# Where the halves of split weights and of the activations lie, modulo 128 bytes

## The reference

```python
x = first_block(x, c, ...)     # modulation from c, indexed attention, stick-breaking attention,
                               # gated merge, then peer_ffn: keys pick 16 experts per head
x = second_block(x, mem, ...)  # conv + blocked attention + gated linear attention,
                               # cross attention on mem, then a convolved gated FFN of width 2752
```

```python
proj = hn @ w_in[l]                                  # many column blocks: w_qi, w_qb, w_g, ...
qh = (h @ w_q)                                       # w_pq
pre = jnp.einsum('cd,chkd->chk', hc, u[ec])          # computed here for all 16384 experts: u
return jnp.einsum('chk,chkd->cd', coef, v[ec])       # likewise: v, with most coefficients zero
u = causal_dwconv(h @ w_up, ...); ... @ w_down       # w_up, w_dn
```

## Time and profile before

| what | value |
|---|---|
| median of three runs | 1450.76 us (1448.74 to 1456.02) |
| the profiled execution, its own time | 1450.47 us |
| its span, first to last instruction | 1448.7 us |
| granted TensorE clock, mean | 0.988 of full |
| PE busy | 1401.2 us, 97% of the span |
| DVE, ACT, POOL busy | 1097.8, 836.1, 360.9 us |
| share of PE in the chain that ended last | 81% |

### The profile page before, as it was taken

The page is one execution under the profiler, slowest core; times in us unless marked ns, Lnnn a source line. Parts: engine busy times, 40 slices in busy tenths (PEclk is TensorE's granted clock), DMA queues, the critical chain, the costliest instruction groups (busy, mean ns, idle before and its releaser), DMA issues.

```text
span 1448.7 us, 25878 instructions
## 1 busy us (share of the span) xinstructions
PE 1401.2 (97%) x10406; PEld 1301.1 (90%) x10406; DVE 1097.8 (76%) x1903; ACT 836.1 (58%) x1447; POOL 360.9 (25%) x227
## 2 busy tenths in 40 slices
PE   7999999899998999999999999999999999899997
PEld 5998899899998999999988888887889899799997
DVE  7788887567889888999756666677667667797762
ACT  4554774444454677777645445465546666776651
POOL 3216101234445100000032222344322221433200
PEclk9999999899999999999999999999999999999999
DMA  9757775455664544444557666665666536285630
GB/s 386 269 190 268 247 240 176 161 159 179 190 184 146 174 148 147 147 146 146 154 179 221 192 193 196 212 196 181 194 200 245 186 107 199 75 260 176 193 114 30
DMA packets 73721, 268.24 MB, mean 185 GB/s; under 512 B 8401, under 2 KB 9730, under 8 KB 72834
## 3 DMA queue, kind: packets, MB, share of 16 engines
q1 hardware_dynamic: 71280, 256.41, 56.1%
q10 hardware_dynamic: 1426, 7.56, 1.5%
q0 software_dynamic: 896, 2.62, 0.5%
HBM read 262.88 MB, written 3.67 MB: 184 GB/s over the span
## 4 chain that ended last, share of the span: by engine, by line
PE 81%; DVE 12%; ACT 4%; issue 1%; DMA 1%; POOL 1%; DVEq 0%; ACTq 0%; POOLq 0%
PE bank L611 80%; DVE split L1825 3%; DVE ada_acc L1860 2%; ACT split L1295 1%; DVE PR L2275 1%; DMA ringb<-in_w_ada 1%; DVE PR L2272 1%; POOL H L2644 0%; PE bank L784 0%; POOL split L2617 0%; DVE H L2366 0%; DVE PR L2280 0%; DMA vecs<-in_vecs 0%; DVE PA L2076 0%; DVE MH L1927 0%
## 5 line engine op out<-in xcount | busy, mean ns | idle before, releaser
L611 PE MATMUL bank<-H,split 128*128 128x256 f32 x5928 | 732.8, 282 | 15.9 <-DVE split L1825 7.7
L611 PEld LDWEIGHTS bank<-H,split 128*128 128x128 f32 x5928 | 710.2, 189 | 23.5 <-DVE split L1825 9.9
L1295 ACT CAST split<-ringb 128x1024 fp32r<-128x1024 f32 x350 | 365.9, 1047 | 284.5 <-PE bank L611 270.7
L2617 POOL TENSOR_TENSOR split<-ringb,split 128x1024 fp32r<-128x1024 f32 x91 | 229.0, 2517 | 665.7 <-ACT split L1295 665.7
L611 PE MATMUL bank<-split,H 128*128 128x512 f32 (+1 forms) x1728 | 391.1, 388 | 3.3 <-DVE H L2366 1.8
L1825 DVE TENSOR_TENSOR split<-ringb,split 128x1024 fp32r<-128x1024 f32 x259 | 330.9, 1280 | 77.5 <-ACT split L1295 77.4
L611 PEld LDWEIGHTS bank<-split,H 128*128 128x128 f32 x1728 | 321.3, 188 | 71.2 <-POOL split L2617 2.5
L2366 DVE TENSOR_TENSOR H<-PR,H 128x256 fp32r<-128x256 f32 x128 | 137.1, 1074 | 105.5 <-ACT H L1634 105.4
L1825 DVE TENSOR_TENSOR split<-far,split 128x1024 fp32r<-128x1024 f32 x77 | 99.7, 1303 | 33.5 <-ACT split L1295 33.4
L1295 ACT CAST split<-far 128x1024 fp32r<-128x1024 f32 x89 | 92.7, 1047 | 55.1 <-PE bank L611 43.9
L1610 ACT ACTIVATE PR<-bank 128x512 f32<-128x512 f32 (+31 forms) x59 | 28.7, 486 | 76.3 <-PE bank L611 76.3
(11 more groups left out here) (298 smaller groups left out, 1264.0 us busy)
## 6 DMA issues: line engine op xcount, KB each, us to landing
ringb<-in_u SPq DMA_DIRECT2D x128, 512.0 KB, 3.7
ringb<-in_v SPq DMA_DIRECT2D x128, 512.0 KB, 4.4
ringb<-in_w_ada SPq DMA_DIRECT2D x28, 512.0 KB, 5.3
far<-in_w_up SPq DMA_DIRECT2D x26, 512.0 KB, 4.2
far<-in_w_ada SPq DMA_DIRECT2D x20, 512.0 KB, 5.3
ringb<-in_w_up SPq DMA_DIRECT2D x17, 512.0 KB, 4.8
ringb<-in_w_pq SPq DMA_DIRECT2D x16, 512.0 KB, 3.8
far<-in_w_dn SPq DMA_DIRECT2D x14, 512.0 KB, 4.2
```

The costliest lines, as they stand in the source:

```text
L611: return TE.matmul(o, l, r, start=start, stop=stop, skip_group_check=True)
L1295: S.copy(buf(m)[0], slots[P.slot[m]]).then_inc(hi_done, 1)
L2617: G.tensor_tensor(lo, slots[P.slot[m]], hi.bitcast(F32), ALU.subtract).then_inc(lo_g, 1)
```

## The change

The pair 0 stays as it is, with both parts in the even half. The pair 1 gets its low part in the odd half, and the pair 2 its high part. The low part of `H` moves to the even half, while its high part stays in the odd half. `cf` stays in the even half of its 128 bytes. 16 floats are added to `split` and 16 to `H`, and `PA` is 32 floats shorter, so that what follows `PA` in the same phase does not move; tensors between are shifted by 64 bytes (`xT`) or by 128 bytes (all others, which leaves them as they were modulo 128). The order of the instructions on every engine, and what each waits for, is the same as before; only addresses differ.

```diff
-        split = sb("split", [128, 3, 2, UNIT], F32R)
+        split = sb("split", [128, 6 * UNIT + 16], F32R)
         xT = sb("xT", [128, 8, T])
 
-        H_all = sb("H", [128, 16 + 16 * T], F32R)
-        H = H_all[:, 16:16 + 16 * T].rearrange("p (z k t) -> p z k t", z=2, k=8)
+        H_all = sb("H", [128, 32 + 16 * T], F32R)
+        H = H_all[:, 0:32 + 16 * T].rearrange("p (z r) -> p z r", z=2)[:, :, 0:8 * T].rearrange("p z (k t) -> p z k t", k=8)
...
-            PA = sb("PA", [128, 20624], where=ph)
+            PA = sb("PA", [128, 20592], where=ph)
...
-        Hf = H_all[:, 0:16 * T]
+        Hf = H_all[:, 16:16 + 16 * T]
...
-        bufs = [(split[:, i, 0, :], split[:, i, 1, :]) for i in range(3)]
+
+        bufs = [(split[:, hi:hi + UNIT], split[:, lo:lo + UNIT])
+                for hi, lo in ((0, UNIT), (2 * UNIT, 4 * UNIT + 16), (5 * UNIT + 16, 3 * UNIT))]
```

## The result

The changed kernel takes 1463.2 us (median of 5, 1461.88 to 1465.0), against 1450.76 for the kernel before: a ratio of 1.0081 as estimated from all runs of both, with a 95% interval of 1.0062 to 1.01. The time lies in the stated range of 1430 to 1468 and at the price given for the rival "the switches are dear" (1463.5), but the forecast was a small gain to 1446.8, and 1463.2 lies outside the 1440 to 1454 that the text had allowed its own case.

A forecast was written before the change was run, and what follows sets the result against it. PE, with no idle time in these stages, was taken to bound the kernel by its matmul step. Terms -11.3 - 0.5 + 3.0 + 4.8 = -4.0 us gave 1446.8 us, own range 1440 to 1454, stated range 1430 to 1468.

The forecast's parts named there:

- the switches are dear: Rival: in alternating stages each switch of halves costs the full 4.5 ns, +12.7 us, 1463.5 us; chance 0.31.
- What bounds the kernel: Whole kernel: PE is busy 97% of the span, and in these stages only one matmul's step sets the pace.
- Which addresses go with which pace: PE's matmul rows: same-half pairs are free, unlike mostly held, 4.5 ns slower per 256 columns, 6.6 per 512.
- Term 1: Lin stages with `H`: 2510 matmuls become like and come free at 4.5 ns each, -11.3 us.
- Term 2: Stages moving `Ym`, `act_t`, `Ya`, `Yb`, `MH`: 222 pairs become like, half counted at 4.5 ns, -0.5 us.
- Term 3: Stage `v` and the `lin_nat` stages: 456 pairs net become unlike at 6.6 ns each, +3.0 us.
- Term 4: Moving stream of `H` stages, `v` and its like: 4781 switches of halves at 1 ns, +4.8 us.
- Term 5: ACT, DVE and POOL writing or reading buffers now in other halves, `xT` shifted 64 bytes: priced at nothing.
- Addresses do nothing: Rival: the pace is set by how a row starts, not by likeness; 1450.8 us, chance 0.16.
- Like pairs reset the pace: Rival: in `H` stages like pairs free the whole row, -24.3 us, with switches +4.8, 1431 us; chance 0.15.

The follow-up runs named there:

- e10: Kernel before with `cf` moved 64 bytes on and nothing else moved; 1461.63 us, ratio 1.0071.
- e3: Kernel before with a pad between `split` and `xT` that shifts all tensors behind `split` by 128 bytes; 1440.67 us, ratio 0.9934.
- e7: Kernel before with `cf` moved by 128 bytes, and the later stages' tensors shifted by 128 bytes with it; 1455.38 us, ratio 1.0015.
- e4: Kernel before with both parts of `H` in the even half, at the weights' own place; 1459.92 us, ratio 1.0062.
- e6: Changed kernel with `cf` moved by 128 bytes, back to 128 modulo 256; 1459.36 us, ratio 1.0048 to the kernel before.
- e2: Kernel before with only the `H` half of the change: low part of `H` in the even half; 1453.4 us, ratio 1.0017.
- e1: Kernel before with only the buffers' half of the change, `cf` at 0 modulo 256, `H` both parts odd; 1453.47 us, ratio 1.0008.
- e11: Kernel before with `cf` moved 192 bytes on, stages behind `v` at the addresses of e7; 1450.76 us, ratio 1.0002.
- e12: The same program as e5 run once more, against the kernel before; 1433.68 us, ratio 0.9871.
- e5: Kernel before with `H` moved on by 128 bytes, `cf` at 0 modulo 256, later stages' buffers 128 bytes further; 1434.7 us, ratio 0.9866.

## Why the prediction was wrong

- *What bounds the kernel.* Right. PE had no idle time to give or take in these stages, and a change of its step by some nanoseconds went fully into the time, in both directions. That addresses can set the step was right too: e10 moves one loaded operand by 64 bytes and `v` gets 10 us longer. By the Trainium skill's page "SBUF — State Buffer", section "Who interferes with whom", PE's two reads go through independent ports and PE never waits on anyone; the 233.3 against 226.7 ns of e10 don't agree with the reading that addresses then cost nothing. What waits there the runs don't show; they show that the step depends on where PE's two operands start.
- *Which addresses go with which pace.* **The step that failed.** The text said "call a pair like if both start in the same half of 128 bytes" and "like has been free wherever it occurs in a long row". The half is not the quantity: e3 and e7 change no half and move stages by 4 to 9 us. The place modulo 256 sorts the even rows, and what a row ran before it counts as well. And like was seen only with 512 columns; carried to 256 columns it has the wrong sign, 120.0 ns instead of 113.3 (e4). The trace of before held a warning that I didn't use: `Ya`, and `act_t` behind its idle moment, ran free, `H` was held, all unlike, and by the program's addresses the first two lie at -64 and `H` at +64.
- *Term 1, -11.3 us* for 2510 like pairs in lin stages with `H`. It came out at +3.6 us busy. In the changed kernel no pair's units come free in `u` (117.9, 117.8 and 118.7 ns), and the slowest are those that the rule called like three times; the mean of 118.1 mixes distances of 0, 64 and 128.
- *Term 2, -0.5 us.* `w_dn` alone became 1.1 us slower; by the starts, steps at distance 0 take 119 to 120 ns there, and `act_t` itself now lies 128 bytes further.
- *Term 3, +3.0 us* for unlike pairs in `v`. It measured 7.4 us along the chain. `cf` stayed in its half and was counted as unchanged, but moved from 128 to 0 modulo 256, and that alone costs 8.8 us (e7). The new places of the buffers alone cost 4.3 us (e6), near the term, but by luck: the loss lies in the units of pairs 0 and 1, and pair 2, in which most of it was looked for, took 226.7.
- *Term 4, +4.8 us* for switches. e2 has almost 4000 of them and its `u` step is 117.8, as before, so with 256 columns they cost nothing net. For the 826 of `v` and its like no run has them alone. The two observations at 1127.67 and 1092.13 us were also changes of distance, not only of halves.
- *Term 5, nothing* for other engines. Right: DVE and ACT are busy within 0.3 us of before.
- *The rivals.* "Dear switches" gave the right time for a wrong reason. "Addresses do nothing" fell. "Like pairs reset the pace" has a true core: in e1 the units with the addresses of before ran free, and in `w_up` a row that has come free at -64 stays free at +64. But it was not the like pairs that did it, and in the changed kernel nothing came free.

What stays open: why the distance has this order for 256 columns and another for 512, what picks the pace at a row's start at +64 or -64, and why the two halves of the change, 1.0008 and 1.0017 by themselves, give 1.0081 together. The last is seen in `u`, where e1 gained 1.5 ns per matmul and the changed kernel, which has `H`'s low part moved too, did not. That the loss of the changed kernel comes from the operands' places is shown, in `v` also by parts; how unlike buffers in one ring act on each other's steps is not.

## What to carry to other kernels

When PE streams without idle time, compute the step from long rows of the timeline and compare it across stages of the same form; here a spread of 3 to 6% at one granted clock came with addresses, and was worth a try. Then vary one operand's place by 64 bytes at a time over 256, and the 256-column and 512-column stages apart, since -64 is the best place for one and the worst for the other. Moving `H` by 128 bytes, and with it the later stages' buffers, gave 1.3% here. A row's pace can also depend on the buffers before it, so look at the steps buffer by buffer and not at the mean alone. And a tensor shifted "harmlessly" by 128 bytes behind an edit is part of the edit.

## What had not been expected of the hardware

- A shift of 128 bytes of everything behind one tensor, with no instruction changed, was worth -0.7% (e3).
- Rows of over 900 identical matmuls keep one of two paces, 113.3 or 117.8 ns, to a nanosecond or two per matmul. `act_t` went from one to the other at an idle 0.53 us, and `w_up` in e11 with no idle time, at a change of buffer from +64 to -64.
- The same program ran its gated stage in 246.06 and in 252.45 us in two executions on two chips (e12, e5), while its long rows agreed. Part of the scatter of single times, 1431.65 to 1437.44 us in e5, may come from there; this was not shown.
